# First layer of a two-block transformer kernel: square sums next to the token tiles, modulation tile by tile, two weight chunks in places of their own, and modulation blocks between the first products

## What is computed

```python
shift, scale, gate = jnp.split((c_act @ w_mod + b_mod)[:, None, :], 3, axis=-1)
shift_c, scale_c, gate_c = jnp.split(cc_act @ w_mod + b_mod, 3, axis=-1)
lat = split_cols((rms_norm(h, norm_g) * (1.0 + scale) + shift) @ w_in)
cx = split_cols((rms_norm(hc, norm_g) * (1.0 + scale_c) + shift_c) @ w_in)
```

## Time and profile before

| | before |
|---|---|
| three runs | 1839.61, 1842.37, 1842.48 us; median 1842.37 |
| profiled execution | 1841.66 us; span in the trace 1839.8 us |
| mean granted TensorE clock | 0.979 of full speed |
| busy in the span: PE, DVE, ACT, POOL | 1701.1, 839.7, 712.4, 606.2 us |
| bytes moved | 152.20 MB, mean 83 GB/s |

### The profile page before, as it was taken

How to read it: one execution, slowest core, us unless ns; L and a number is a source line. 1 busy time by engine, 2 the same in 40 slices (tenths; PEclk the granted TensorE clock), 3 DMA queues, 4 the chain that set the end, 5 groups by cost and what they waited for, 6 DMA issues and landing times.

```text
span 1839.8 us, 32525 instructions
## 1 busy us (share of the span) xinstructions
PE 1701.1 (92%) x13658; PEld 1370.7 (74%) x13658; DVE 839.7 (46%) x1513; ACT 712.4 (39%) x1101; POOL 606.2 (33%) x318
## 2 busy tenths in 40 slices
PE   6899999988989989989999988788899899999997
PEld 3788888866878767768877757686688688888886
DVE  0401265475330356476747567574434444444113
ACT  3525213254353524354634966014423522222222
POOL 0222322193323323453034304113235244444443
PEclk9899999999999999999999989999999999999999
DMA  8344311210122111403522200001121132222232
GB/s 335 127 163 146 115 48 47 106 46 13 64 96 69 58 58 59 138 1 102 178 88 92 80 24 2 4 2 54 58 73 47 51 107 95 92 93 102 94 104 78
DMA packets 43721, 152.20 MB, mean 83 GB/s; under 512 B 4544, under 2 KB 7744, under 8 KB 43328
## 3 DMA queue, kind: packets, MB, share of 16 engines
q1 hardware_dynamic: 40032, 140.73, 22.1%
q10 hardware_dynamic: 3552, 9.47, 1.4%
HBM read 145.98 MB, written 4.19 MB: 82 GB/s over the span
## 4 chain that ended last, share of the span: by engine, by line
PE 78%; DVE 11%; ACT 6%; issue 4%; DMA 1%; SPq 0%; POOL 0%; DVEq 0%; ACTq 0%
PE wide_ps L1900 53%; PE wide_ps L1957 4%; PE pair_ps L2012 2%; PE wide_ps L2192 1%; PE wide_ps L1973 1%; PE wide_ps L2495 1%; DVE xn L1383 1%; DMA ring<-weights 1%; DVE xn L1628 1%; DVE proj L1301 1%; PE duo_ps L1995 1%; PE duo_ps L2622 1%; DVE proj L1297 1%; PE wide_ps L2078 1%; PE wide_ps L2603 1%
## 5 line engine op out<-in xcount | busy, mean ns | idle before, releaser
L564 POOL TENSOR_TENSOR ring_r<-ring,scratch_r 128x1024 fp32r<-128x1024 f32 x176 | 430.9, 2449 | 961.9 <-ACT scratch_r L736 887.5
L1900 PE MATMUL wide_ps<-xn_r,scratch_r 128*128 128x512 f32 x1272 | 470.3, 370 | 0.0
L1900 PE MATMUL wide_ps<-work_r,scratch_r 128*128 128x512 f32 (+1 forms) x1109 | 427.5, 386 | 5.2 <-ACT proj L723 5.2
L1900 PE MATMUL wide_ps<-work_r,ring_r 128*128 128x512 f32 (+1 forms) x1109 | 412.6, 372 | 0.0
L736 ACT ACTIVATE scratch_r<-ring 128x1024 fp32r<-128x1024 f32 x192 | 203.6, 1061 | 529.4 <-PE wide_ps L1900 461.5
L1900 PEld LDWEIGHTS wide_ps<-xn_r,scratch_r 128*128 128x128 f32 x1272 | 240.4, 189 | 47.5 <-issue 5.4
L1900 PEld LDWEIGHTS wide_ps<-work_r,scratch_r 128*128 128x128 f32 x1109 | 209.0, 188 | 53.5 <-ACT proj L723 9.9
L1900 PEld LDWEIGHTS wide_ps<-work_r,ring_r 128*128 128x128 f32 x1109 | 209.1, 189 | 38.6
L1900 PE MATMUL wide_ps<-proj_r,scratch_r 128*128 128x512 f32 (+1 forms) x662 | 225.7, 387 | 2.5 <-DVE proj_r L1249 2.5
L1900 PEld LDWEIGHTS wide_ps<-proj_r,scratch_r 128*128 128x128 f32 x662 | 125.4, 190 | 30.7 <-DVE proj_r L1249 3.3
L723 ACT ACTIVATE proj<-wide_ps 128x512 f32<-128x512 f32 (+2 forms) x86 | 56.7, 659 | 208.1 <-PE wide_ps L1900 198.4
(11 more groups left out here) (442 smaller groups left out, 2972.6 us busy)
## 6 DMA issues: line engine op xcount, KB each, us to landing
ring<-weights SPq DMA_DIRECT2D x256, 512.0 KB, 3.5
h<-tokens SPq DMA_DIRECT2D x4, 768.0 KB, 11.5
h<-tokens ACTq DMA_DIRECT2D x1, 3072.0 KB, 10.0
out<-h ACTq DMA_DIRECT2D x1, 2048.0 KB, 7.2
h<-out ACTq DMA_DIRECT2D x1, 2048.0 KB, 9.2
out<-h SPq DMA_DIRECT2D x16, 128.0 KB, 1.7
const_sb<-const SPq DMA_DIRECT2D x1, 1089.0 KB, 6.0
h<-mem ACTq DMA_DIRECT2D x1, 1024.0 KB, 12.7
```

Source lines behind the costliest of these rows:

```text
L564: pool.tensor_tensor(as_r(wt), wt, as_r(w_lead(m)).bitcast(F32), ALU.subtract).then_inc(w_split, 1)
L1900: last = pe.matmul(bank[:, a:b], wt[:, cols], as_r(x[:, a:b]), start=n == 0 and p == 0, stop=n == len(k_order) - 1 and p == 2)
```

## The change

It has four parts. The squares and their sums follow the arriving tokens, two feature tiles at a time, and most modulation blocks come behind them. The columns of `w_mod` are reordered on the host, so that block b holds shift and scale of feature tile b; DVE forms them block by block (`first_modulation`) and ACT's `modulate` waits for one tile's at a time. The chunks of the first two projection tiles leave the stream and the ring and get transfers and places of their own in `proj` (`w_home`). And `project_two` of the first layer has modulation blocks between its steps: blocks 6 and 7, and the late blocks 8 and 9. Besides, the constants come in two transfers, the small one (`ident`, `ones`, `pick`) early, and `mod_row_ps` uses the free `pair_ps` for blocks 4 to 7.

```diff
@@ chunk_plan and where @@
-    for name, n in ([("mod0", MOD_FIRST), ("proj0", NPROJ + 2 * MIXED), ("dft0", FOURIER_CHUNKS[0]), ("out0", KT),
+    for name, n in ([("mod0", MOD_FIRST), ("proj0", NPROJ - 2 + 2 * MIXED), ("dft0", FOURIER_CHUNKS[0]), ("out0", KT),
...
-        return PLAN["proj0"] + (4 + n if n < 2 else 3 * n + 2 if n < MIXED else 2 * MIXED + n)
+        return PLAN["end"] + n if n < 2 else PLAN["proj0"] + (3 * n if n < MIXED else 2 * MIXED + n - 2)
@@ PSUM rows and places @@
+        def mod_row_ps(ly, b):
+
+            if ly == 0 and b < 4:
+                return wide_ps[:, b % 2, 0:2 * P]
+            if ly == 0 and b < KT:
+                return pair_ps[:, 512 * (b % 2):512 * (b % 2) + 2 * P]
+            return duo_ps[:, 768:1024]
...
+        ROWS_BEHIND = {0: 4, 1: 5, 2: 6, 3: 7, 5: KT, 7: KT + 1}
...
+        def w_home(stage, n):
+
+            if stage == "proj0" and n < 2:
+                return flat[:, 8 * TOK + CHUNK * n:8 * TOK + CHUNK * (n + 1)]
+            return ring[:, where(stage, n) % RING, :]
@@ SP @@
                 if c == 0:
-                    sp.dma_start(const[:, :], const_d).then_inc(const_landed, 16)
+                    sp.dma_start(const[:, 0:CONST_HEAD], const_d[:, 0:CONST_HEAD]).then_inc(const_landed, 16)
+                if c in (5, 6):
+                    sp.dma_start(w_home("proj0", c - 5), weights[where("proj0", c - 5)]).then_inc(first_landed[c - 5], 16)
+                if c == 7:
+                    sp.dma_start(const[:, CONST_HEAD:], const_d[:, CONST_HEAD:]).then_inc(tables_landed, 16)
@@ ACT, modulate @@
-                act.wait_ge(mod_ready, (2, 4)[ly])
                 for k in range(KT):
-                    if ly == 0 and k == 1:
-                        modulation_row(KT + 1)
-                        weight_leads("proj0", 1)
+                    act.wait_ge(mod_ready, (2 * (k + 1), 2 * KT + 2)[ly])
                     act.wait_ge(scaled, 8 * ly + k + 1)
...
+                    if ly == 0 and k in ROWS_BEHIND:
+                        modulation_row(ROWS_BEHIND[k])
@@ ACT, start @@
                     for k in range(KT):
-                        modulation_row(k)
+                        if k in (0, 4):
+                            modulation_row(k // 4)
                         act.wait_ge(tokens_landed[k // 2], 16)
                         square(0, k, h[:, k, :], TOK)
                     mean_root(0, TOK)
-                    weight_leads("proj0", 0)
-                    modulation_row(KT)
+                    weight_leads("proj0", 0, 2)
+                    modulation_row(2)
+                    modulation_row(3)
@@ DVE @@
+            def first_modulation(b):
+
+                dve.wait_ge(mod_turned, b + 1)
+                bias = prm["b_mod"][:, b:b + KT + 1:KT].unsqueeze(2).broadcast_to([P, 2, 2])
+                dve.tensor_tensor(mod[:, 0, b:b + KT + 1:KT], first_mod_ps(b).rearrange("p (n s) -> p n s", s=2)[:, b:b + KT + 1:KT], bias, ALU.add).then_inc(mod_ready, 1)
+                dve.wait_ge(mod_ready, 2 * b + 1)
+                dve.scalar_tensor_tensor(out=mod_scale[:, 0, b], in0=mod[:, 0, KT + b], scalar=1.0,
+                                         in1=prm["norm_g"][:, b:b + 1].broadcast_to([P, 2]), op0=ALU.add, op1=ALU.mult).then_inc(mod_ready, 1)
...
-            modulation(0)
+            first_modulation(0)
+            first_modulation(1)
...
                         dve.tensor_tensor(xn_t[:, k, :], h[:, k, :], root[:, :], ALU.mult).then_inc(scaled, 1)
+                    if ly == 0 and k < KT - 2:
+                        first_modulation(k + 2)
                     if k:
@@ PE @@
-            for b in range(KT):
-                if b >= 2:
-                    pe.wait_ge(mod_row, b - 1)
-                modulation_part(0, 2 * b)
...
+            modulation_part(0, 0)
+            pe.wait_ge(const_landed, 16)
+            modulation_part(0, 1)
+            norm_step(0, 0, TOK)
+            norm_step(0, 1, TOK)
+            modulation_part(0, 2)
+            modulation_turn(0)
+            norm_step(0, 2, TOK)
+            norm_step(0, 3, TOK)
+            modulation_part(0, 3)
+            norm_step(0, 4, TOK)
+            norm_step(0, 5, TOK)
+
+            def first_block(b):
+
+                pe.wait_ge(mod_row, b - 1)
+                if b == 4:
+                    pe.wait_ge(root_ready, 1)
+                modulation_part(0, 2 * b)
+                modulation_turn(b - 1)
+                if b == 2:
+                    norm_step(0, 6, TOK)
+                    norm_step(0, 7, TOK)
+                modulation_part(0, 2 * b + 1)
+
+            for b in range(2, 6):
+                first_block(b)
+
+            pe.wait_ge(mod_row, 4)
...
+            def behind_first_products(k):
+
+                if k < 2:
+                    first_block(6 + k)
+                elif k == 2:
+                    modulation_turn(KT - 1)
+                elif k == 4:
+                    late_block(KT)
+                elif k == 6:
+                    modulation_turn(KT)
+                    late_block(KT + 1)
```

More of the change, by code:

```diff
@@ L205, in build @@
         out_bank = lambda a: pair_ps[:, 512 * a:512 * a + 512]
-        par_landed, const_landed = sem("par_landed"), sem("const_landed")
+        par_landed, const_landed, tables_landed = sem("par_landed"), sem("const_landed"), sem("tables_landed")
+        first_landed, first_used = [sem(f"first_landed{n}") for n in range(2)], sem("first_used")
         tokens_landed = [sem(f"tokens_landed{n}") for n in range(KT // 2)]
@@ L562, in split_weights @@
                         pool.wait_ge(x_split, X_SPLITS[stage] + KT)
-                    wt = ring[:, c % RING, :]
+                    wt = w_home(stage, n)
                     pool.tensor_tensor(as_r(wt), wt, as_r(w_lead(m)).bitcast(F32), ALU.subtract).then_inc(w_split, 1)
@@ L721, in evacuate @@
                 g = EVAC[stage] + tile
-                act.wait_ge(chunk_used, chunks)
+                if stage == "proj0" and tile < 2:
+                    act.wait_ge(first_used, tile + 1)
+                else:
+                    act.wait_ge(chunk_used, chunks)
                 act.activation(dst, wide_ps[0:rows, g % 2 if bank is None else bank, 0:w], func).then_inc(evacuated, 1)
@@ L729, in weight_leads @@
                     c, m = where(stage, i), SPLIT_AT[stage] + i
-                    act.wait_ge(landed[c % RING], 16 * (c // RING + 1))
+                    if stage == "proj0" and i < 2:
+                        act.wait_ge(first_landed[i], 16)
+                    else:
+                        act.wait_ge(landed[c % RING], 16 * (c // RING + 1))
                     last = m - 2
@@ L735, in weight_leads @@
                         act.wait_ge(chunk_used, SPLIT_STREAM[last] + 1)
-                    act.activation(as_r(w_used(stage, w_lead(m))), w_used(stage, ring[:, c % RING, :]), ACT.Copy).then_inc(w_lead_ready, 1)
+                    act.activation(as_r(w_used(stage, w_lead(m))), w_used(stage, w_home(stage, i)), ACT.Copy).then_inc(w_lead_ready, 1)
             def leads_after(stage, tile, following=None):
@@ L1937, in last_close, with project_two @@
                 pe.matmul(ps, cst["ones"], squares(N_FFN_POST)[:, 1, a:b], start=False, stop=True).then_inc(sq_used, 1)
-            def project_two(first, second, lead, rest, w, input_ready, norm=None):
+            def project_two(first, second, lead, rest, w, input_ready, norm=None, between=None, done=chunk_used):
                 banks = []
@@ L1947, in project_two @@
                     rows = 32 if stage == "ab_2" else P
-                    banks.append((proj_bank(stage, tile)[0:rows], as_r(w_lead(m)), as_r(ring[:, where(stage, tile) % RING, :]), rows))
+                    banks.append((proj_bank(stage, tile)[0:rows], as_r(w_lead(m)), as_r(w_home(stage, tile)), rows))
                 for k in range(KT):
@@ L1959, in project_two @@
                         if k == KT - 1:
-                            last.then_inc(chunk_used, 1)
+                            last.then_inc(done, 1)
+                    if between:
+                        between(k)
             def project_ahead(stage, tile, lead, rest, w):
@@ L2288, in _ @@
                         modulation_turn(KT + t - 1)
-                    if ly == 0 and t == 0:
-                        pe.wait_ge(mod_ready, 1)
-                    if ly == 0 and t < MIXED:
-                        if t == 1:
-                            modulation_turn(KT)
-                        for half in range(2):
-                            modulation_part(MOD_BLOCKS[KT + t][0], 2 * MOD_BLOCKS[KT + t][1] + half)
+                    if ly == 0 and 2 <= t < MIXED:
+                        late_block(KT + t)
+                    if ly == 0 and t == 2:
+                        pe.wait_ge(tables_landed, 16)
                     query_key_sums(ly, t)
@@ L2764, in lay_out @@
```

(8 more changed lines are left out.)

56 lines of the change are left out of this document (27 added, 29 removed).

## The result

| | before | after |
|---|---|---|
| runs | 1839.61 to 1844.11 us, median 1842.42 (4) | 1817.43 to 1823.31 us, median 1819.95 (4) |
| ratio | | 0.9883, 95% interval 0.9867 to 0.9899 |
| profiled execution, span | 1841.66, 1839.8 | 1817.43, 1815.6 |
| mean granted clock | 0.979 | 0.979 |

A forecast was written before the change was run, and what follows sets the result against it. PE, without slack from 73 us on, was taken as the bound, so its turn at 73.1 coming at 63.0 saves 10.1 us: 1841.66 to 1831.6, plus 0.7 for the median, put at 1832.0; range 1828 to 1837.

The forecast's parts named there:

- the one on transfers: Constants, chunks and token pairs: earlier landings, tokens by 18.4 us, but the same total moves, no gain or loss.
- the step on the bound: PE, busy 77.00 of 77.00 us from 73 to 150, has no slack, so an earlier mark arrives at the end.
- the mark: PE's turn of a late modulation row behind the first two projection tiles: 73.14 us before, forecast at 63.0.
- The order's term: New order in the first layer: the mark at 63.0 and not 73.1, 10.1 us less.
- To the root: Squares and sums following the arriving tokens: square 0 ends at 9.7 us, root at 29.0 against 46.2.
- The hole: Behind the root, PE waits 3.2 us, from 28.3 to 31.5, for row 2 from ACT.
- The clock: Behind the root, granted clock falls near 31 us and comes back near 37, as PE is busy without a break.
- the rival of the longer low clock: Wait behind the root keeps PE at half clock longer: the mark about 67.6, gain 5.5, 1836.2 us; chance 0.12.
- Products and blocks: Product steps with blocks between, from 38.6 us to the mark at 63.0; step 6 waits for row 8, until 57.2.
- DVE's small pair: Two small DVE operations following each turn, taken as 0.4 us for the pair.
- lockstep: PE, ACT and DVE tied into one ring, no two tiles overlapping: the mark at 94, 1863 us; chance 0.05.
- absorbed gain: A later stage waiting for a transfer or another engine takes up the gain: time stays at 1842; chance 0.06.

The follow-up runs named there:

- before_pad: The before kernel with 62 unused columns appended to the constants, moving the buffers behind them 224 bytes; 1830.08 us, 0.9931 of before.
- after_shift: The after kernel with 8 more unused columns at the end of the constants, moving the buffers behind them 32 bytes; 1835.00 us, 0.9955 of before.
- rows_first_late: rows_first with the row of late block 8 behind the modulation of tile 6 instead of tile 5; 1818.84 us, 0.9873 of before.
- rows_first: The after kernel with ACT's order behind the root: row 2, lead of weight chunk 0, row 3, lead of chunk 1; 1821.82 us, 0.9892 of before.
- early_leads: rows_first_late with both weight leads ahead of the root, rows 2 and 3 directly behind it; 1819.76 us, 0.9878 of before.

## Why the prediction was wrong

**The sum lacked a term.** The step that failed is the one on transfers: "The same total moves; no gain and no loss here", with the constants' new table taken as bytes to be loaded. I read `CONST_HEAD` and the split in two, not that the table's new length moves five buffers behind it. And the step on the bound, that PE "works 77.00 of 77.00 us" behind the mark and so only the mark could move, took busy for incompressible: before and after, PE is busy 150.00 of 150.00 us in the feed-forward stage, with 649 and 663 matmuls. In its place the runs showed 12.9 us by before_pad, of which the traces put 12.2 on the shorter distances, and all of it lost again in after_shift, 15 us above after. It is the larger part of the result, and none of my rivals had it.

**The order's term was mis-sized**, 10.1 against 7.6 at the mark and 7.9 in after_shift. Of the 2.5 us at the mark, 0.6 are there when the first product starts, 1.5 come in step 0 and 0.5 behind it. (The sum as stated, 1841.66 less 10.1 and 0.7 more for the median, gives 1832.3, where 1832.0 was put.) By its steps:
- To the root: 27.69 against 27.2. The squares began 0.8 us later, at 9.61, since tokens landed later than at 8.8; otherwise the ledger holds.
- The hole: 3.03 us against 3.2, ended by an ACT row. Right.
- The clock: it fell near 32, where 31 was said, and came back near 42, not 37. The step that failed is "come back near 37, as PE is then busy without a break": PE was busy without a break from 31.68 on and it stayed at 0.50. Turn 2, parts 7 to 11 and turns 3 and 4 cost what they cost at half clock, and step 0 of the products took 3.56 us (39.20 to 42.76), not 2.1. The first product started at 39.20 against 38.6. That is the rival of the longer low clock, though its price, the mark at 67.6, was too high by 2.1: it had the first product 1.4 us late, where it was 0.6, and 1.5 us more for block 6, which ran at full clock and took 1.68 (42.76 to 44.44).
- Products and blocks: the wait ahead of step 6 was there, 1.00 us, and ended by DVE, as said; rows_first_late confirmed that row 8 made it.
- DVE's small pair: 0.4 us (25.00 to 25.36), right where POOL is idle. Beside POOL's split the second of them took 2.28 us (32.89). The forecast had only casts and splits suffer from POOL.
- The lockstep and the absorbed gain: neither came. The 7.6 us of the mark are still 7.3 some 770 us later.

The Trainium skill, TensorE: Matmul & The Clock Gate, Part 1, says that the throttled clock is the default and that activity releases it. The trace after agrees as far as it goes: behind a wait of 3.03 us the clock was at half, and it came back at 42, when PE had been busy for 10.3 us, the last 2.8 with product steps. rows_first, rows_first_late and early_leads have the clock low for 6.8, 3.4 and 6.8 us near there, so no order that was tried went without.

## What to carry to other kernels

When PE is busy 100% of a stretch, count its matmuls there and read their distance: here the same busy time held 2% more of them. A change of one buffer's length is a change of every buffer behind it, so look at where the buffers start in the built program, and keep the distances of all matmul operands in multiples of 256 bytes, until a run shows that it doesn't matter. A wait of PE can cost more than its length: in all four orders tried, with waits of 1.14 to 3.03 us behind the root, 3.4 to 10.2 us at half clock followed, though no run took the wait away altogether. A step earlier near the start need not show in the time when other stretches vary by as much from one execution to the next. And one pair of traces is no measure of a change: 2.6 of the 24.2 us between these two belonged to one execution.

## What was not expected of the hardware

- Float32r matmuls of 512 columns, back to back with their weight loads, start every 226.7 ns when their SBUF operands lie at multiples of 256 bytes from each other, and every 231 to 233 ns, as a mean, when both `work` and `scratch` are off by 32, 64 or 128 bytes, or one of them by 32. For this kernel that is 12.9 us of 1842 by the medians. With `work` alone off, products kept the short distance where neither they nor their neighbours read it.
- In the first layer, where pieces of 512 and 256 columns alternate, the place gave no gain that the traces show: before_pad, with its mark 0.3 us earlier, was 0.2 us later than before at 183 us.
- TensorE's granted clock stayed at 0.50 through 8.00 us in which PE was busy 8.00 us, with parts (256 columns on 32 columns of the array) and turns (2 columns), and rose only after product steps had begun.
- A VectorE instruction on 128 x 2 values took 2.28 us instead of 0.16 while GpSimd subtracted a weight chunk (32.89 us in the trace after; 1.60 us at 32.08 in rows_first).
